# A two-layer decoder step: the second mixer's norm and the final norm computed by token on 128x5 numbers

## What is computed

```
def rms_norm(x, g):
    xf = x.astype(jnp.float32)
    y = xf * lax.rsqrt(jnp.mean(xf * xf, axis=-1, keepdims=True) + NORM_EPS)
    return (y * g.astype(jnp.float32)).astype(x.dtype)

for i in range(DEPTH):                       # 0: sparse attention, 1: gated DeltaNet
    h = rms_norm(x, p['norm_mix_g'][i])
    proj = h @ (nsa_w_in or gdn_w_in)
    ... token mixer, cross-attention into 256 memory tokens ...
    x = x + jnp.concatenate([o_mix, o_mem], axis=-1) @ p['w_out'][i]
    h = rms_norm(x, p['norm_ffn_g'][i])
    x = x + jnp.square(jax.nn.relu(h @ p['w_up'][i])) @ p['w_down'][i]
y = rms_norm(x, p['final_norm_g'])
```

## Time and profile before

| | us |
|---|---|
| median of three runs | 2008.68 |
| the three runs | 2008.21, 2008.68, 2011.74 |
| profiled execution, its own time | 2009.57 |
| its span, first to last instruction | 2007.8 |
| TensorE matmuls busy | 1913.4 (95%) |
| TensorE weight loads busy | 1544.9 (77%) |
| VectorE busy | 1048.8 (52%) |
| ScalarE busy | 518.5 (26%) |
| GpSimd busy | 39.5 (2%) |
| mean granted clock of TensorE, of full speed | 0.98 |

### The profile page before, as it was taken

The page is one execution under the profiler, slowest core; times in us unless marked ns, Lnnn a source line. Parts: engine busy times, 40 slices in busy tenths (PEclk is TensorE's granted clock), DMA queues, the critical chain, the costliest instruction groups (busy, mean ns, idle before and its releaser), DMA issues.

```text
span 2007.8 us, 26728 instructions
## 1 busy us (share of the span) xinstructions
PE 1913.4 (95%) x10011; PEld 1544.9 (77%) x10011; DVE 1048.8 (52%) x2334; ACT 518.5 (26%) x1286; POOL 39.5 (2%) x48
## 2 busy tenths in 40 slices
PE   7999999999979999999999999899998999999997
PEld 6788555777768888888877787688876888888885
DVE  4441777555565445455437765465546545445444
ACT  2221777233312122100012513333342222210000
POOL 0000000000001000000010000000000000000001
PEclk9999999999979999999999999999988999999998
DMA  5532200565422222222224112200011222222211
GB/s 228 188 129 66 77 1 1 168 199 185 142 105 84 66 82 84 84 84 84 84 98 158 64 55 76 74 1 1 32 40 56 81 85 84 84 84 84 84 63 45
DMA packets 60801, 175.42 MB, mean 87 GB/s; under 512 B 6529, under 2 KB 39442, under 8 KB 47362
## 3 DMA queue, kind: packets, MB, share of 16 engines
q1 hardware_dynamic: 58050, 163.02, 24.1%
q0 software_dynamic: 2624, 10.70, 1.3%
HBM read 160.76 MB, written 12.93 MB: 87 GB/s over the span
## 4 chain that ended last, share of the span: by engine, by line
PE 88%; DVE 5%; ACT 4%; issue 2%; DMA 0%; POOL 0%; DVEq 0%; SPq 0%; POOLq 0%
PE psum L1798 58%; PE psum L1321 5%; PE psum L901 5%; PE psum L974 2%; PE psum L757 2%; ACT sbuf L801 1%; PE psum L738 1%; DVE sbuf L1657 1%; PE psum L934 1%; PE psum L720 1%; PE psum L1776 1%; PE psum L640 1%; PE psum L1431 1%; PE psum L1873 1%; PE psum L1879 1%
## 5 line engine op out<-in xcount | busy, mean ns | idle before, releaser
L1798 PE MATMUL psum<-sbuf 128*128 128x272 f32 x5152 | 1197.5, 393 | 4.5 <-ACT sbuf L2073 1.4
L1798 PEld LDWEIGHTS psum<-sbuf 128*128 128x128 f32 x5152 | 973.8, 190 | 216.1 <-issue 11.3
L1321 PE MATMUL psum<-sbuf 128*128 128x128 f32 (+3 forms) x1020 | 125.7, 279 | 12.4 <-DVE sbuf L1641 5.2
L1321 PEld LDWEIGHTS psum<-sbuf 128*128 128x128 f32 (+3 forms) x1020 | 118.6, 191 | 19.5 <-DVE sbuf L1641 6.0
L2023 ACT ACTIVATE sbuf<-sbuf 128x544 f32<-128x544 f32 x32 | 20.8, 650 | 396.9 <-DVE sbuf L2367 387.5
L2246 DVE TENSOR_TENSOR sbuf<-sbuf 128x512 f32<-128x512 f32 x92 | 63.4, 689 | 81.4 <-PE psum L1798 73.5
L901 PE MATMUL psum<-sbuf 128*128 128x256 f32 x448 | 105.0, 384 | 0.0
L901 PEld LDWEIGHTS psum<-sbuf 128*128 128x128 f32 x448 | 81.7, 187 | 15.4 <-issue 1.2
L2250 DVE TENSOR_TENSOR sbuf<-sbuf 128x512 f32<-128x512 f32 x92 | 63.8, 693 | 52.1 <-PE psum L1798 50.5
L1500 ACT ACTIVATE sbuf<-psum 128x384 f32<-128x384 f32 (+2 forms) x84 | 40.2, 480 | 106.0 <-PE psum L1321 80.9
L2259 DVE TENSOR_TENSOR sbuf<-sbuf 128x512 f32<-128x512 f32 x92 | 63.1, 686 | 0.0
(11 more groups left out here) (387 smaller groups left out, 2067.2 us busy)
## 6 DMA issues: line engine op xcount, KB each, us to landing
sbuf<-in_w SPq DMA_DIRECT2D x100, 1024.0 KB, 4.9
sbuf<-in_pages SPq DMA_DIRECT2D x256, 128.0 KB, 2.4
sbuf<-in_mcache SPq DMA_DIRECT2D x2, 4096.0 KB, 15.5
sbuf<-in_win SPq DMA_DIRECT2D x8, 512.0 KB, 4.5
out_win_o<-sbuf POOLq DMA_DIRECT2D x8, 512.0 KB, 2.9
sbuf<-in_state SPq DMA_DIRECT2D x6, 512.0 KB, 6.4
out_state_s<-sbuf POOLq DMA_DIRECT2D x6, 512.0 KB, 3.1
sbuf<-in_x SPq DMA_DIRECT2D x1, 2176.0 KB, 12.0
```

Source lines behind the costliest of these rows:

```text
L1321: last = mm(bank(pair[x])[0:rows, width * (h - h0):width * (h - h0 + 1)], lhs(h), rhs(h), start=True, stop=True)
L1798: ins = mm(to, lhs(k), rhs(k), start=first and k == 0, stop=k == 3, skip_group_check=True)
```

## The change

For n = 2 and n = 4 the operands of the sums are exchanged. The squares become the weights and one column of ones is what moves through the array, so that the sums of 128 tokens come out as a column of 128 numbers, one token to a partition. Five blocks of 128 tokens (the last one begins at 416 and overlaps the one before) make 128x5 numbers for `sq_sum` in bank 6, and 128x5 for tile 7 in bank 7. VectorE adds the two, ScalarE takes the root of 128x5, VectorE the reciprocal of 128x5. Then TensorE spreads them over the partitions again: the weights are one column of the reciprocals repeated 128 times, what moves is the identity, and the result is the reciprocal root of each token on all partitions, in banks 6 and 7. VectorE's eight products read it from there rather than from `rstd`. The other three norms keep their form.

Since banks 6 and 7 are then read by VectorE while `single` runs, `single` of layer 1 writes banks 4 and 5 (`both(3 - l)`), and its copy on ScalarE reads them there. The scores of the memory attention use banks 4 and 5 and so wait for that copy (`act_out`).

```diff
+        BLOCKS = (0, P, 2 * P, 3 * P, TT_ - P)
+        SPREADS = ((0, 0, P), (1, P, 2 * P), (2, 2 * P, HALF), (2, HALF, 3 * P), (3, 3 * P, TP), (4, TP, TT_))
+        rms_t, rstd_t = rstd[:, 0:5], rstd[:, 8:13]
...
+            def token_norm_sums(n):
+
+                pe.wait_ge(sq_added, 6 * n)
+                for ci, at in enumerate(BLOCKS):
+                    mm(bank(6)[:, ci:ci + 1], sq_sum[:, at:at + P], ones[:, 0:1], start=True, stop=True)
+                pe.wait_ge(sq_ready, (n + 1) * KT)
+                for ci, at in enumerate(BLOCKS):
+                    last = mm(bank(7)[:, ci:ci + 1], sq[:, 1, at:at + P], ones[:, 0:1], start=True, stop=True)
+                last.then_inc(sq_used, 1)
+                pe.wait_ge(dve_step, RSTD_READY[n])
+                for ci, lo, hi in SPREADS:
+                    half, at = lo // HALF, BLOCKS[ci]
+                    last = mm(both(3)[:, half, lo - HALF * half:hi - HALF * half],
+                              rstd_t[:, ci:ci + 1].to_broadcast([P, P]), ident[:, lo - at:hi - at], start=True, stop=True)
+                last.then_inc(pe_step, 1)
+
             def single(name, l):
...
-                        last = mm(both(3)[:, half, :], view(ring[slot], KT, 256)[:, k, 0:P], halves_of(hT[:, k, :])[:, half, :],
+                        last = mm(both(3 - l)[:, half, :], view(ring[slot], KT, 256)[:, k, 0:P], halves_of(hT[:, k, :])[:, half, :],
...
-                norm_sums(n)
+                token_norm_sums(n)
...
                         if l:
+                            pe.wait_ge(act_out, 2)
                             pe.wait_ge(in_mkv1, 16)
...
             def root(n):
-                act.wait_ge(sq_used, KT + n)
-                f(halves_of(rstd), both(3), ACT.Sqrt, bias=C["eps"], scale=1.0 / D).then_inc(std_ready, 1)
+                if n in RSTD_READY:
+                    act.wait_ge(dve_step, MS_READY[n])
+                    f(rms_t, rms_t, ACT.Sqrt, bias=C["eps"], scale=1.0 / D).then_inc(std_ready, 1)
...
-                f(halves_of(tile), both(3), ACT.Copy).then_inc(act_out, 1)
+                f(halves_of(tile), both(3 - l), ACT.Copy).then_inc(act_out, 1)
...
             def norm(n, gain):
+                if n in RSTD_READY:
+                    dve.wait_ge(sq_used, KT + n)
+                    own(dve.tensor_copy(rms_t, bank(6)[:, 0:5]))
+                    tt(rms_t, rms_t, bank(7)[:, 0:5], ALU.add).then_inc(dve_step, 1)
                 dve.wait_ge(std_ready, n + 1)
-                own(dve.reciprocal(rstd, rstd))
+                if n in RSTD_READY:
+                    dve.reciprocal(rstd_t, rms_t).then_inc(dve_step, 1)
+                    dve.wait_ge(pe_step, RSTD_SPREAD[n])
+                else:
+                    own(dve.reciprocal(rstd, rstd))
+                over = both(3) if n in RSTD_READY else halves_of(rstd)
                 for k in range(KT):
-                    stt(out=hT[:, k, :], in0=xT[:, k, :], scalar=gain[:, k:k + 1], in1=rstd, op0=ALU.mult,
-                        op1=ALU.mult).then_inc(h_ready, 1)
+                    stt(out=halves_of(hT[:, k, :]), in0=halves_of(xT[:, k, :]), scalar=gain[:, k:k + 1], in1=over,
+                        op0=ALU.mult, op1=ALU.mult).then_inc(h_ready, 1)
```

More of the change, by code:

```diff
@@ L330, in build @@
         pe_step, dve_step = sem("pe_step"), sem("dve_step")
-        MEM_SS, VG_DONE, PKV_DONE, BA_DONE, GT_DONE, LENGTHS_DONE = 1, 2, 3, 4, 5, 6
-        GATE_PRE, GATES_READY, GEXP_PRE = 1, 2, 3
+        MEM_SS, VG_DONE, PKV_DONE = 1, 2, 3
+        BA_DONE, GT_DONE, LENGTHS_DONE = 5, 6, 7
+        RSTD_SPREAD = {2: 4, 4: 8}
+        GATE_PRE, GATES_READY, GEXP_PRE = 3, 4, 5
+        MS_READY, RSTD_READY = {2: 1, 4: 6}, {2: 2, 4: 7}
         pe_out = sem("pe_out")
@@ L2008, in root @@
             def root(n):
-                act.wait_ge(sq_used, KT + n)
-                f(halves_of(rstd), both(3), ACT.Sqrt, bias=C["eps"], scale=1.0 / D).then_inc(std_ready, 1)
+                if n in RSTD_READY:
+                    act.wait_ge(dve_step, MS_READY[n])
+                    f(rms_t, rms_t, ACT.Sqrt, bias=C["eps"], scale=1.0 / D).then_inc(std_ready, 1)
+                else:
+                    act.wait_ge(sq_used, KT + n)
+                    f(halves_of(rstd), both(3), ACT.Sqrt, bias=C["eps"], scale=1.0 / D).then_inc(std_ready, 1)
             def first_norm():
@@ L2064, in silu_gates, with inputs_out @@
                 f(c, c, ACT.Silu).then_inc(conv_done, 1)
-            def inputs_out(name, units, tile, pair, after_p1, after_p5, after):
+            def inputs_out(name, l, units, tile, pair, after_p1, after_p5, after):
                 act.wait_ge(pe_out, obase[name] + 1)
-                f(halves_of(tile), both(3), ACT.Copy).then_inc(act_out, 1)
+                f(halves_of(tile), both(3 - l), ACT.Copy).then_inc(act_out, 1)
                 for U in range(ubase[name], ubase[name] + units):
@@ L2196, in pair @@
                     return gproj[:, GQ + 2 * (g - 1):GQ + 2 * g, :] if g < 10 else gz[:, 2 * (g - 10):2 * (g - 9), :]
-                inputs_out("gdn_in", GDN_U, gproj[:, BA, :], pair, after_p1, after_p5, after)
+                inputs_out("gdn_in", 1, GDN_U, gproj[:, BA, :], pair, after_p1, after_p5, after)
                 act.wait_ge(ks_read, 1)
@@ L2209, in _ @@
             memory_kv()
-            inputs_out("nsa_in", NSA_U, proj[:, GT, :], lambda g: proj[:, 2 * g:2 * g + 2, :], lambda g: None,
+            inputs_out("nsa_in", 0, NSA_U, proj[:, GT, :], lambda g: proj[:, 2 * g:2 * g + 2, :], lambda g: None,
                        lambda g: None, memory_attention(0))
```

## The result

| | before | changed |
|---|---|---|
| median, us | 2009.20 | 2006.19 |
| lowest to highest, 22 runs each | 2006.12 to 2011.74 | 2004.30 to 2009.87 |
| profiled execution, its span | 2007.8 | 2004.5 |
| ratio to before (95% interval) | | 0.9986 (0.9980 to 0.9992) |

The change makes the kernel faster by 0.14%, 2.8 us by the ratio, with an interval of 1.6 to 4.0 us. The median lies 0.4 us under the forecast of 2006.6. That forecast started from a median of 2008.68; from the 2009.20 measured here the forecast saving of 2.1 us would give 2007.1. So the number was right within 1 us; the parts of which it was made were not all right, as the traces show.

The account below looks back on a forecast made before the run. TensorE, busy 95% of the span, was taken as the bound, with waits at two norms. Savings of 1.24 + 1.23 - 0.35 = 2.1 us from the 2008.68 median gave 2006.6 us, range 2003.8 to 2009.6.

Parts of the forecast that it names:

- The sums: TensorE, start of each changed norm: ten one-column matmuls, 20 records at 0.119 us plus a 0.13 tail, 2.51 us.
- The tiny operations: Between sums and spread: VectorE copy and sum with hops 0.45 us, root 0.26, reciprocal 0.19, hop to TensorE 0.13.
- The spread: TensorE, behind the reciprocal: six matmuls, 12 records, with one repeated column as weights, 1.66 us.
- The products: VectorE's eight products reading PSUM in two pieces: no extra cost, bounds 0 and 0.2 us an operation.
- Rival C: Products from PSUM are dearer at the end of the program: 1.6 us back, 2008.2 us; chance 0.1.
- The final norm: End of the program, from the start of the sums to the first product: 1.23 us less than 6.47.
- The clock in the mixer's norm: Around the second mixer's norm: clock falls as before, in part earlier, 0.35 us against the saving; bounds +1.65 and -2.8.
- rival B: Clock falls before the spread in both norms and stays low through half the tile: 1.6 us more, 2010.3; chance 0.13.
- Rival A: Clock holds in the second mixer's norm, saving 1.65 us more: 4.1 us less in all, 2004.6; chance 0.17.

Follow-up runs that it names:

- the control: The changed kernel itself run once more, beside runs of the kernel before on the chip of the last experiments: ratio 0.9990 (0.9981 to 0.9999).
- changed kernel with filled stops: Against the changed kernel, two unread wide matmuls behind the sums and two behind the spread in the second mixer's norm; ratio to before 0.9990 (0.9981 to 0.9999).

## Why the prediction was right, and where it was not

**The sums.** Forecast 2.51 us, measured 2.41 in the mixer's norm (1.28 + 1.13). Less the same tail of 0.13 that is 0.114 a record: the lower of the two values that I had named, where I took 0.119.

**The tiny operations.** Forecast from the end of the sums to the start of the spread 0.03 + 0.42 + 0.26 + 0.19 + 0.13 = 1.03 us, measured 0.98. The root takes 0.31 where I took 0.23 from 128x30; the hop to TensorE 0.04 where I took 0.13. The two errors nearly cancel.

**The spread.** Forecast 1.66, measured 1.55 in the final norm and 1.52 to 1.54 where the clock was full throughout. Repeating one column as weights costs nothing: its 12 weight loads take 1.41 us, 0.118 each, and the ten of the sums 1.19, 0.119 each.

**The products.** Forecast at no extra cost, against an estimate of 65 ns each from the Trainium skill's fixed terms. Measured 778 ns for 780. Rival C is out: the eight take 5.62 us for 5.66. The longer fixed term for PSUM that the Trainium skill gives ("VectorE: DVE Perf Modes", the section on the TRN2 errata) does not show here, where only one of the two tensors moved to PSUM; the measurement decides.

**The final norm.** 1.23 us forecast, 1.49 measured. The sums, the tiny operations and the spread, each a little shorter than forecast, explain it.

**The clock in the mixer's norm.** This is the part of the forecast that failed. I wrote "I take it that the clock falls as before" and put 0.35 us against the saving. It did fall, but at the start of the spread and not behind it, which is the place that I had given to rival B. The spread cost 1.23 us more than at full clock, and the tile stayed at 9.1 us. Of 1.5 us that the chain saves at full clock 0.2 were left. So the term was 1.3 and not 0.35. B's full price did not come, for in the final norm the clock held until the spread was all but done in this trace, and the tile was slower than before by 0.1 us only. In other executions it does not hold there either (the kernel with the sums added in PSUM, 2.30; that with wide sums alone, 2.61).

**The sum.** Forecast 2.1 us, of which 0.9 in the mixer's norm and 1.2 in the final one. The traces show 0.2 and 1.5, 1.7 in all, and the times 2.8 (1.6 to 4.0). The total was near because one part was 0.7 too large and the other 0.3 too small, and because the times show 1.1 us more than the steps; that is luck. Whether these 1.1 us are real stays open: the trace's sum lies inside the interval, and the control (0.9990, 2.0 us) is nearer to it. Both traces of the changed kernel are of executions with a mean granted clock of 0.979. Nine of its 22 executions had 0.981; none of these was profiled, and in them the mixer's norm may have kept its clock.

**Rival A**, the clock that holds, did not come in the trace either, but its price was right: when the clock is made to hold, the tile takes 7.57 to 7.61 us and the spread 1.52 to 1.54, and 13.55 us remain of the 16.44 of before. That is 2.9 us less, and I had given it 1.24 + 1.65 = 2.9 there. Against the changed kernel it is 2.7.

## What to carry to other kernels

A shorter chain beside a waiting TensorE is worth its length only if the clock that TensorE works at behind it is the same. When you replace wide matmuls by narrow ones in such a place, read the granted clock around it in both traces before you book the gain; where weight loads set the pace, a wider moving operand is free and may hold the clock. And when a saving is below the spread of single executions, measure it as a step between two instructions in the trace, and add up the steps, before you believe a ratio.

## What the runs showed of the hardware

The clock came down without a pause of TensorE in front of it. In the changed kernel with filled stops the engine waited 0.6 us for GpSimd ahead of the sums, as in all these kernels, and then went from one-column sums (2.4 us) into wide matmuls (1.0 us) and the spread without a gap; and the spread ran at 1.2 GHz (2.74 us). With the same instructions and 64 columns in the sums it stayed at 2.4 GHz. That is one pair of traces. The Trainium skill ("TensorE: Matmul & The Clock Gate", the part on the warmup) ties the fall to an idle stretch; the kernel before shows such a fall, within a pause of 5.3 us, and the filled one shows a fall without such a stretch.

A second condition is where the norm stands in relation to the clock's own changes. All five traces with one-column sums in the mixer's norm start them 464.1 to 464.3 us behind the end of the same earlier low stretch, and in all five the clock fell. The two with wide sums and filled stops stand there too (464.2), and it held. The two with wide sums and empty stops stand at 462.8 and 463.1, so that their mixer's norms do not show that width alone would do. The final norms come nearer to it. Counted from the end of the low stretch ahead of them (at 1525 to 1529 us), three stand at about one place: wide sums with a stop of 1.00 us (464.0), in which the clock fell within the spread (2.61 us); one-column sums with a stop of 0.58 us (464.1), in which it fell as well (2.30 us); and wide sums with a stop of 0.58 us (463.9), in which it held (1.52 us). So the narrow sums and the stop both count, on three traces. No run moved a norm on purpose.

The clock also goes with most of the difference between executions of one and the same program. The 22 executions of the changed kernel fall into three groups without overlap: nine from 2004.30 to 2005.84 us with a mean granted clock of 0.981, ten from 2005.97 to 2007.52 with 0.979, three from 2009.62 to 2009.87 with 0.977. The start of the mixer's sums lies between 1046.4 and 1053.3 us in the thirteen traces, with nothing ahead of it that the kernels do in another way but for the two pieces of the first norm's products (783 ns for 780). The traces of before and of the changed kernel differ there by 1.54 us: 0.6 us are there at 19 us of the span, and the rest is the sum of steps of 1.2 to 1.7 us both ways, each in a stretch in which one of the two has more low clock (210 to 225, 260 to 275, 310 to 325 and 350 to 365 us). In the latest of them, the kernel with 64-wide sums added in PSUM, the attention of the samples ran at the low clock from about 491 to 501 us; in the kernel before it did not. By that stretch alone it falls back 4.6 us (ScalarE's instructions are 0.8 us ahead of the other trace's at 490 us and 3.8 behind at 507). The same stretch of both (columns as above, PEclk the third from the end), before first:

```profile
495.00:500.00 5.00, 4.92 (x28) 2.54 (x28) 0.86 (x5) 2.48 (x6) 0.00 (x0) 1.00 0.79 231
```

```profile
495.00:500.00 5.00, 5.00 (x20) 2.56 (x21) 0.36 (x2) 2.18 (x5) 0.00 (x0) 0.50 0.60 149
```

So whether a low-clock stretch falls on a place is partly a matter of the single execution. This is why the final norm's spread took 1.5 us in some of the traces and 1.7 to 2.6 in others, and why a change that only shortens a pause has no single price.
